# A hybrid encoder layer on one Trainium2 core: the square sums of its norms on four 32-column tiles, and one more product to add them

## The reference, cut to what matters

```python
def rmsnorm(x, g):
    y = x * lax.rsqrt(jnp.mean(x * x, axis=-1, keepdims=True) + EPS)
    return y * g

mk, mv = memory_kv(mem, ...)                    # rmsnorm(mem) @ wk, @ wv, 256 memory frames
x = x + 0.5 * swiglu_ffn(rmsnorm(x), ...)       # FFN 1
x = x + token_mixers(rmsnorm(x), ...)           # band attention and gated delta rule
x = x + cross_attention(rmsnorm(x), mk, mv)
x = x + 0.5 * swiglu_ffn(rmsnorm(x), ...)       # FFN 2
y = rmsnorm(x)
```

## Time and profile before

| | |
|---|---|
| median of 3 runs | 3475.68 us (3475.59 to 3482.91) |
| the profiled execution | 3480.32 us, its span 3478.5 us |
| mean granted TensorE clock | 0.983 |
| PE busy | 3293.7 us, 95% |
| ACT, DVE, POOL busy | 674.7, 1288.3, 954.7 us |
| sums at L479, third of x | 15 times 16 instructions of 384 columns |
| sums at L479, memory | 16 instructions of 256 columns |

### The profile page before, as it was taken

How to read it: one execution, slowest core, us unless ns; L and a number is a source line. 1 busy time by engine, 2 the same in 40 slices (tenths; PEclk the granted TensorE clock), 3 DMA queues, 4 the chain that set the end, 5 groups by cost and what they waited for, 6 DMA issues and landing times. The chain is left out here.

```text
span 3478.5 us, 50346 instructions
## 1 busy us (share of the span) xinstructions
PE 3293.7 (95%) x19945; PEld 3129.6 (90%) x19945; DVE 1288.3 (37%) x2289; ACT 674.7 (19%) x1302; POOL 954.7 (27%) x436
## 2 busy tenths in 40 slices
PE   6999999999999999988988979999799999999998
PEld 5999999999889888877887879988599999999997
DVE  3232333332445545642442454232225323233324
ACT  5100000000132422433333332123311000000001
POOL 3433333333313123101001023221123333333331
PEclk9999999999999999989999999999899999999999
DMA  5411111111232133112112144024401111111111
GB/s 181 141 37 48 42 42 42 42 36 43 83 109 107 77 119 117 60 69 80 71 38 93 45 157 156 21 96 156 147 31 43 43 48 40 42 40 41 36 48 55
DMA packets 96556, 254.24 MB, mean 73 GB/s; under 512 B 11552, under 2 KB 52640, under 8 KB 93728
## 3 DMA queue, kind: packets, MB, share of 16 engines
q1 hardware_dynamic: 45568, 146.95, 12.3%
q10 hardware_dynamic: 50848, 105.25, 8.4%
HBM read 199.83 MB, written 52.33 MB: 72 GB/s over the span
## 5 line engine op out<-in xcount | busy, mean ns | idle before, releaser
L124 POOL TENSOR_TENSOR w_hi<-w_raw,zero 128x1024 fp32r<-128x1024 f32 x201 | 385.4, 1917 | 2231.3 <-PE psum L155 1320.0
L155 PE MATMUL psum<-x_hi,w_hi 128*128 128x384 f32 x3024 | 598.2, 338 | 51.5 <-DVE x_lo L2136 32.2
L155 PE MATMUL psum<-x_lo,w_hi 128*128 128x384 f32 x3024 | 592.4, 335 | 0.0
L155 PE MATMUL psum<-x_hi,w_lo 128*128 128x384 f32 x3024 | 589.5, 334 | 0.0
L155 PEld LDWEIGHTS psum<-x_hi,w_hi 128*128 128x128 f32 x3024 | 533.6, 189 | 58.1 <-issue 47.6
L155 PEld LDWEIGHTS psum<-x_lo,w_hi 128*128 128x128 f32 x3024 | 533.9, 189 | 0.0
L155 PEld LDWEIGHTS psum<-x_hi,w_lo 128*128 128x128 f32 x3024 | 530.8, 188 | 0.0
L127 POOL TENSOR_TENSOR w_lo<-w_raw,w_hi 128x1024 fp32r<-128x1024 f32 x201 | 500.0, 2488 | 15.8
L394 DVE TENSOR_TENSOR f_hid<-psum,f_gate 128x384 f32<-128x384 f32 x132 | 73.6, 558 | 861.8 <-PE psum L155 859.3
L349 ACT ACTIVATE f_gate<-psum 128x384 f32<-128x384 f32 x132 | 64.7, 493 | 1477.4 <-PE psum L155 1477.4
L155 PE MATMUL psum<-f_h_hi,w_hi 128*128 128x384 f32 x1056 | 269.1, 335 | 0.0
(11 more groups left out here) (276 smaller groups left out, 3354.2 us busy)
## 6 DMA issues: line engine op xcount, KB each, us to landing
w_raw<-units SPq DMA_DIRECT2D x224, 512.0 KB, 3.5
gate_dram<-b_stash ACTq DMA_DIRECT2D x48, 192.0 KB, 1.9
e_gate<-gate_dram ACTq DMA_DIRECT2D x48, 192.0 KB, 2.5
a_kc<-k_cache ACTq DMA_DIRECT2D x4, 2048.0 KB, 7.5
a_vc<-v_cache ACTq DMA_DIRECT2D x4, 2048.0 KB, 13.9
x_sk<-mem_k ACTq DMA_DIRECT2D x8, 1024.0 KB, 8.5
proj_dram<-a_cv ACTq DMA_DIRECT2D x12, 576.0 KB, 2.8
b_pad<-proj_dram SPq DMA_DIRECT2D x12, 576.0 KB, 4.8
```

Of the source, the lines that this page charges most:

```text
L124: pool.tensor_tensor(k.w_hi[s][:, :], k.w_raw[s][:, :], k.zero[:, 0:1].to_broadcast([P, D]), ALU.add)\
L155: mm = pe.matmul(out, wl if part == 2 else wh, (xl if part == 1 else xh)[:, n0:n1], start=(part == 0 and i == 0), stop=(part == 2 and i == ...
```

## The change

`sums` keeps its eight matmuls of squares but gives each only 32 columns of ones, and sends chunk c to the column tile 32 * (c % 4) of the array, so that four matmuls address four different tiles. The bank then holds, in each of four groups of 32 rows, the partial sum over two chunks, 32 times over. A new step `gather` copies the bank with ScalarE to `rinv`; a new step `total` multiplies this by the whole 128x128 matrix of ones, which adds the four partial sums and spreads them. Each is counted 32 times, so the logarithm is scaled by 1 / (32 * D). The wait for a free `rinv` moves from `root` to `gather`.

`total` is put between the first and the second of the three parts of the product that follows the sums (`between` in `product`), in the FFN tails after the next short product, and in the memory stage two units later; there `root` and `upper` move one unit later on ScalarE (units 5, 7, 9 instead of 4, 6, 8). In the last norm and the memory's own norm nothing lies between sums and total.

```diff
-def product(pe, out, tiles, n0, n1):
+def product(pe, out, tiles, n0, n1, between=None):
...
     for part in range(3):
+        if part == 1 and between:
+            between()
...
@@ ffn_phase, tensor @@
-                mm = product(pe, k.ps[g % NPS][:, 0:THIRD], tiles, n * THIRD, (n + 1) * THIRD)
+                mm = product(pe, k.ps[g % NPS][:, 0:THIRD], tiles, n * THIRD, (n + 1) * THIRD,
+                             (lambda: norm.total(pe, 2)) if order is by_third and g == 2 else None)
...
                     if isinstance(i, int) and i == LAST and n >= 1 and d == 4:
                         tail.sums(pe, n - 1)
+                    if isinstance(i, int) and i == LAST and n >= 1 and d == 5:
+                        tail.total(pe, n - 1)
@@ ffn_phase, scalar @@
         tail.square(act, 0)
+        tail.gather(act, 0)
         tail.root(act, 0)
         third_added(1)
         tail.square(act, 1)
         if tail.out is None:
             tail.upper(act, 0)
+        tail.gather(act, 1)
         tail.root(act, 1)
@@ Norm @@
-            mm = pe.matmul(k.ps[4 + n][:, 0:self.width], k.ones[:, :], self.squares[:, c, self.cols(n)],
-                           start=(c == 0), stop=(c == KD - 1))
-        mm.then_inc(s.ntotal.sem, 1)
+            r = 32 * (c % 4)
+            mm = pe.matmul(k.ps[4 + n][r:r + 32, 0:self.width], k.ones[:, 0:32], self.squares[:, c, self.cols(n)],
+                           start=(c < 4), stop=(c >= 4), tile_position=(0, r))
+        mm.then_inc(s.nparts.sem, 1)
+
+    def total(self, pe, n):
+
+        k, s = self.k, self.s
+        pe.wait_ge(s.ngathered.sem, s.ngathered.at(n + 1))
+        pe.matmul(k.ps[4 + n][:, 0:self.width], k.ones[:, :], self.rinv[:, n % 2, :], start=True, stop=True)\
+            .then_inc(s.ntotal.sem, 1)
+
+    def gather(self, act, n):
+
+        k, s = self.k, self.s
+        act.wait_ge(s.nparts.sem, s.nparts.at(n + 1))
+        if n >= 2:
+            act.wait_ge(s.nscaled.sem, s.nscaled.at(2 * (n - 1)))
+        act.activation(self.rinv[:, n % 2, :], k.ps[4 + n][:, 0:self.width], ACT.Copy).then_inc(s.ngathered.sem, 1)
 
     def root(self, act, n):
         k, s = self.k, self.s
         act.wait_ge(s.ntotal.sem, s.ntotal.at(n + 1))
-        if n >= 2:
-            act.wait_ge(s.nscaled.sem, s.nscaled.at(2 * (n - 1)))
         r = self.rinv[:, n % 2, :]
-        act.activation(r, k.ps[4 + n][:, 0:self.width], ACT.Ln, bias=k.eps[:, 0:1], scale=1.0 / D)\
+        act.activation(r, k.ps[4 + n][:, 0:self.width], ACT.Ln, bias=k.eps[:, 0:1], scale=1.0 / (32 * D))\
@@ last_norm_phase @@
     def tensor(pe):
         norm.sums(pe, 2)
+        norm.total(pe, 2)
@@ memory_phase @@
-    pe_norm = {3: [lambda pe: norm.sums(pe, 0)], 5: [lambda pe: norm.sums(pe, 1)], 7: [lambda pe: norm.sums(pe, 2)]}
+    pe_norm = {3: [lambda pe: norm.sums(pe, 0)], 5: [lambda pe: norm.total(pe, 0), lambda pe: norm.sums(pe, 1)],
+               7: [lambda pe: norm.total(pe, 1), lambda pe: norm.sums(pe, 2)], 9: [lambda pe: norm.total(pe, 2)]}
     act_norm = {0: [lambda act: norm.square(act, 0)], 1: [lambda act: norm.square(act, 1)],
-                2: [lambda act: norm.square(act, 2)], 4: [lambda act: norm.root(act, 0), lambda act: norm.upper(act, 0)],
-                6: [lambda act: norm.root(act, 1), lambda act: norm.upper(act, 1)],
-                8: [lambda act: norm.root(act, 2), lambda act: norm.upper(act, 2)]}
+                2: [lambda act: norm.square(act, 2)], 4: [lambda act: norm.gather(act, 0)],
+                5: [lambda act: norm.root(act, 0), lambda act: norm.upper(act, 0)], 6: [lambda act: norm.gather(act, 1)],
+                7: [lambda act: norm.root(act, 1), lambda act: norm.upper(act, 1)], 8: [lambda act: norm.gather(act, 2)],
+                9: [lambda act: norm.root(act, 2), lambda act: norm.upper(act, 2)]}
@@ residual_phase @@
-            product(pe, k.ps[j % NPS][:, 0:THIRD], tiles, n * THIRD, (n + 1) * THIRD).then_inc(k.dense_done.sem, 1)
+            product(pe, k.ps[j % NPS][:, 0:THIRD], tiles, n * THIRD, (n + 1) * THIRD,
+                    (lambda: tail.total(pe, SUMMED[j - 1])) if j - 1 in SUMMED else None).then_inc(k.dense_done.sem, 1)
...
             tail.square(act, n)
+            tail.gather(act, n)
             tail.root(act, n)
...
```

More of the change, by code:

```diff
@@ L360, in scalar @@
             norm.square(act, 2)
+            norm.gather(act, 2)
             norm.root(act, 2)
@@ L441, in __init__ @@
         self.nsq, self.ntotal = k.counter(name + "_squared"), k.counter(name + "_total")
+        self.nparts, self.ngathered = k.counter(name + "_parts"), k.counter(name + "_gathered")
         self.nln, self.nrinv = k.counter(name + "_ln"), k.counter(name + "_rinv")
@@ L533, in tensor @@
             self.sums(pe, n)
+            self.total(pe, n)
     def lower_both(self, dve, n):
@@ L547, in scalar @@
         for n in range(self.nb):
+            self.gather(act, n)
             self.root(act, n)
@@ L566, in done @@
         s, nb = self.s, self.nb
-        for sig, n in ((s.nsq, 2), (s.ntotal, 1), (s.nln, 1), (s.nrinv, 1), (s.nscaled, 2)):
+        for sig, n in ((s.nsq, 2), (s.nparts, 1), (s.ngathered, 1), (s.ntotal, 1), (s.nln, 1), (s.nrinv, 1), (s.nscaled, 2)):
             sig.base += n * nb
@@ L910, in turn_streams, with job @@
             mm.then_inc(k.ys_turned.sem, 1)
-        def job(i, g, u, n):
+        def job(i, g, u, n, between=None):
             if n == 0:
@@ L918, in job @@
                       xh[:, c, :], xl[:, c, :]) for c in range(KD)]
-            product(pe, k.ps[g % ND][:, 0:THIRD], tiles, n * THIRD, (n + 1) * THIRD)\
+            product(pe, k.ps[g % ND][:, 0:THIRD], tiles, n * THIRD, (n + 1) * THIRD, between)\
                 .then_inc(k.dense_done.sem, 1)
@@ L930, in first_jobs @@
                 for u in range(3):
-                    job(0, 3 * n + u, u, n)
+                    job(0, 3 * n + u, u, n, (lambda: norm.total(pe, 2)) if n == 0 and u == 1 else None)
                     if n == 0 and u == 0:
@@ L2419, in tensor @@
                      for c in range(KD)]
-            product(pe, k.ps[g % 2][:, 0:THIRD], tiles, n * THIRD, (n + 1) * THIRD).then_inc(k.dense_done.sem, 1)
+            product(pe, k.ps[g % 2][:, 0:THIRD], tiles, n * THIRD, (n + 1) * THIRD,
+                    (lambda: norm.total(pe, 2)) if g == 2 else None).then_inc(k.dense_done.sem, 1)
             if g == 1:
```

## The result

| | before | after |
|---|---|---|
| median of 5 runs each, same chip | 3479.18 us (3475.59 to 3482.91) | 3461.18 us (3457.27 to 3465.28) |
| the profiled execution | 3480.32, span 3478.5 | 3458.65, span 3456.9 |
| mean granted TensorE clock | 0.983 | 0.981 |

The ratio is 0.9946, with a 95% interval of 0.9932 to 0.9959: 18.0 us less by the medians, 21.6 by the two spans. The forecast was 3455 with a range of 3437 to 3466 and 20.5 us less; the time lies in the range, 6 us above the forecast. The kernel before ran at 3479.2 in this comparison, so 3.5 of these 6 us are its own run to run difference.

What follows compares the result with a forecast made beforehand. PE, busy 95%, was taken as the bound, except where ScalarE, VectorE or GpSimd takes over. Place by place 1.2 + 0.8 + 4.4 + 2.5 + 0 + 4.0 + 7.6 = 20.5 us, 3475.7 to 3455; 8 in 10 between 3437 and 3466.

Steps and rivals of the forecast that it cites:

- Tiled sums, 1.6 us: Each third's sums on four tiles: 1.6 us on PE instead of 5.16, including 0.2 for entering and leaving the tiles.
- The hidden length: Eight 512-column instructions on four tiles: 0.16 of the modelled length hidden, 0.88 us to the next start.
- The upper bound: Sums priced by four matmuls in a row on one tile, 0.144 us each: 3.45 us.
- Rival C: The tiles do not run together, sums cost 5 us: 3489 us; chance 0.03 slower, 0.05 no difference.
- `total` and copy: Per third, `total` 0.65 us on PE and copy 0.58 us on ScalarE, with no PE wait where ScalarE is free.
- Memory stage: ScalarE bounds it, so PE's gain is worth nothing: -0.8 us, with ends at -5 and +4.
- End of FFN 1, attention: -4.4 us at FFN 1's end, with PE waiting about 1.4 us at `total`, and -2.5 in attention.
- Mix to cross and wo to FFN 2: `scale` chunks and GpSimd's splits take turns, PE idles 5.8 us in wo: -4.0 us for mix, 0 for wo.
- rival B: PE idle stretches at three places bring the slower clock, 1.7 us each, memory stage 4 us later: 3465 us, chance 0.13.
- Last norm: Squares to logarithm at the kernel's end: 4.14 us becomes 2.35, -1.8.
- the start: Memory's own norm 1.8 us earlier, limited by the first weight unit's landing: -1.2 us.
- Rival A: Nearly all of PE's gain arrives, at about 3435 us (3430 to 3444); chance 0.17.

Runs made afterwards that it cites:

- experiment 1: Changed kernel with chunks 2r and 2r + 1 on tile r, one behind the other, instead of taking turns over four tiles: 3463.98 us, ratio 0.9957 to the kernel before.
- experiment 9: Changed kernel with four chunks on the first tile and four on the second, copy and `total` on 64 rows: one run, 3486.78 us beside 3479.76.
- experiment 3: Changed kernel with the memory stage's three thirds as before (whole-array sums, no copy, no `total`): 3460.75 us, ratio 0.9947 to the kernel before.
- experiment 7: Experiment 4 with the copy of third 1's sums put between the halves of third 0's `upper` in FFN 1's tail: 3449.21 us, ratio 0.9926.
- experiment 2: Changed kernel with sums on the whole array again, copy and `total` kept: 3499.98 us, ratio 1.0073 to the kernel before.
- experiment 4: Changed kernel with third 1's last `scale` chunks put behind the additions they held up in the residual stages: 3452.5 us, ratio 0.9919 to the kernel before.
- experiment 5: Kernel before, with third 1's last `scale` chunks put behind the additions in the residual stages: 3479.47 us, ratio 1.0000.

## Why the prediction was right, and where its terms were off

*Tiled sums, 1.6 us.* Right, in both parts: 1.43 to the next start, as the rows gave, and 0.20 in the six matmuls behind, 1.24 instead of 1.04, where I had put 0.2 for going into the tiles and out again. That the 0.20 comes from the tiling is not shown; a `total` over 32 rows has the same 0.22 behind it. The hidden length that I read from rows 4 as 0.16 is 0.19; nothing rests on it. The upper bound was wrong as a bound for another order: L2370 has eight in a row on a tile (experiments 1, 9), and two chunks in a row would have cost 0.02 us. Rival C is out: one tile alone costs 5.28 us, and 16 instructions in 1.5 us are only possible with all four at work. The rule of the Trainium skill (TensorE: Matmul & The Clock Gate, "The mechanism") that weights load under a running matmul only in another row group doesn't agree with these rows: all tiles here lie in the same row group. The Trainium skill (TensorEngine Tiling (Array Packing), "Key Properties") says that different tiles load weights and multiply in parallel, and the traces agree with that: 16 instructions in 1.43 us, where one tile alone takes 5.28.

*`total` and copy.* `total` 0.65, copy 0.49 instead of 0.58. Where ScalarE was free PE didn't wait, as predicted.

*Memory stage.* -1.8 for -0.8, and -2.7 in the second trace, inside -5 to +4. Two units and a third of the norm take ScalarE 12.4 us (59.45 to 71.88) against 12.5 before. I counted 1 us more a third for the copy; with the copy in it the stretch is no longer than before. So this term was wrong, and the sum came near in part by luck. That PE's gain is worth nothing here was right (experiment 3).

*End of FFN 1, attention.* -7.1 for -6.9. PE's wait at `total` was 0.78 us, not 1.4; its cause, the copy behind both halves of `upper`, was as stated (experiment 7).

*Mix to cross and wo to FFN 2.* The mechanism was right. Against the offset of the stage, GpSimd started 4.7 us earlier (4.8 predicted), `scale` 3.3 (3.4), and PE idled 5.16 us (5.8). The work behind it came back at +0.4 us where I had -0.3. Seven chunks were not "done or begun" when GpSimd started, as I had read the earlier trace rows: six were, and the seventh began 0.15 us after it (2612.41) and took 2.25. Then 1.5 us went to the slower clock, 797.34 instead of 795.84 us in the long row. I had named this loss (up to 2 us) and not put it into the sum. But it belongs to this execution: the second trace of the changed kernel has the same wait ahead of the sums, 5.13 us, and its long row is

```profile
2629.09 795.84 PE psum L157 x4590
```

There the place comes to -0.2, for a forecast of 0. In mix to cross it was -4.4 us at the product that waited, and 1.5 back while the first matmuls there took 2.4 us for 8 instead of 1.55; in the second trace it was -2.9 and the same 1.5 back. Both are rival B's mechanism, which had the right places and the right size of 1.7, and the wrong part in the memory stage.

*Last norm.* -0.3 for -1.8, in both traces, the term that failed most for its size. I took the pieces at full clock. The window before, and then that of the changed kernel:

```profile
3459.00:3467.00 8.00, 5.70 (x18) 2.96 (x16) 4.79 (x9) 2.96 (x3) 0.00 (x0) 1.00 0.25 90
```

```profile
3438.00:3446.00 8.00, 4.53 (x18) 0.86 (x18) 4.74 (x9) 4.06 (x5) 0.00 (x0) 0.64 0.45 163
```

PE has nothing to do there but the sums and `total`, it idles 2.17 us ahead of the sums and 0.61 ahead of `total`, and at a granted clock of 0.64 `total` takes 1.66 us instead of 0.65. From the end of the squares to the logarithm it is 3.86 us, where it was 4.14 and I had 2.35. Shortening work in a stretch without other work left PE with less to do there, and `total` runs at the slower clock in all five traces with the sums in turn over four tiles; in the other four traces that have a `total`, it takes 0.91 us here. But the 4.14 us of before are no fixed measure either. Experiment 5 has the same sums in this place and a granted clock of 0.79, and its logarithm comes 1.7 us later:

```profile
3460.64 0.58 ACT L489 ACTIVATE n_rinv<-psum,eps 128x384 f32<-128x384 f32 x1 [5.83 <-PE psum L479]
```

Against that trace the changed kernel gains 2.0 us here, so how much of the missing 1.5 us the median contains stays open.

Without the 3.8 us in the unchanged stretch, and 0.5 more of the same kind in cross, the profiles differ by 17.3 us, next to the medians' 18.0; the second trace, without the same two stretches, gives 18.1. The 3.2 us missing to my 20.5 are, by the first trace, wo to FFN 2 (1.9), the last norm (1.5) and mix to cross (1.1), less 1.3 from the start and the memory stage. By the second 2.4 are missing: mix to cross (2.7), the last norm (1.5) and the start (0.4), less 2.3 from the memory stage, FFN 1 and wo to FFN 2. The total is firmer than its parts: some of them were off in opposite ways, and that 20.5 came within 2.5 us of the medians' difference is in part luck.

Rival A fell: PE was given 36 us, and half of it arrived. What took the rest: VectorE and GpSimd at the two residual stages, with the slower clock around PE's wait (shown by experiments 2, 4 and 5); the memory stage, which doesn't go by PE (experiment 3; that ScalarE bounds it is read, not tested); and the clock in the last norm, which the traces show and no run removed.

## What to carry to other kernels

A change that shortens work on the busiest engine and adds a round trip over another one moves two things: the engine's own work, and the distance between that chain and everything that hangs on the engine directly. Here the second was worth 25 us against the 38 of the first, and most of it sat at two places where `scale` met GpSimd's splits; count such distances first, then put the waiting additions ahead of the work that collides (9 to 12 us more, experiments 4 and 7). With several column tiles, keep to four instructions in a row on one tile, the most that was seen to cost nothing; within that the order is free. And price a shortened piece by the clock of its own stretch, not by the clock of a busy one.

## What the runs showed of the hardware that I had not expected

- A 32-column tile is no faster than the whole array: by the chain, 16 instructions of 384 columns take 5.28 us on one tile, 5.16 on 128 columns, 4.02 on two tiles with eight in a row each, 1.45 on four with four in a row, 1.43 on four in turn. With tiles the six whole-array matmuls behind take 1.24 to 1.26 us, without 1.04.
- `total` over fewer rows is slower: 0.65 us over 128 rows, 0.84 over 32 or 64, with 0.22 more in the products behind it.
- The same instructions of one kernel take up to 6.5 us more or less over 1200 us, at granted clocks of 0.66 to 1.00 in stretches of 10 us, and the same last norm, from squares to logarithm, took 4.14 us in the trace of before and 5.83 in that of experiment 5. A difference of two spans is no better than that.
